# Leaving the first product of a column block whole instead of dividing it into two column parts

## The reference

```
proj   = rms_norm(x) @ w_in                    # 1024 -> 10 x 1024
y_conv = (silu(zc) * bg * conv(cg * xc)) @ w_out_conv
y_attn = (silu(za) * attention(q, k, v)) @ w_out_attn
x      = rms_norm(x + (g_conv * y_conv + g_attn * y_attn) @ w_o)
for layer in (0, 1):                           # second block
    mix = concat(attention(x @ w_in...), memory_attention(x, mem)) @ w_out
    x   = layer_norm(ALPHA * x + mix)
    a, b = split(x @ ffn_w_in)                 # 1024 -> 2 x 2816
    x   = layer_norm(ALPHA * x + (gelu(conv(a)) * b) @ ffn_w_out)   # 2816 -> 1024
```

## Time and profile before

| | |
|---|---|
| time, median of 3 runs | 921.16 us (921.1 to 921.88) |
| time of the profiled execution | 921.2 us |
| its span, first to last instruction | 919.5 us |
| mean granted TensorE clock | 0.997 |
| PE busy | 906.9 us, 99% of the span |
| VectorE (DVE), ScalarE (ACT) busy | 648.1 us, 524.4 us |
| divided first products recorded (L1684) | 36 |

### The profile page before, as it was taken

One profiled execution on the slowest core, in us unless ns is written; L12 is line 12 of the kernel. 1 busy time (PEld: TensorE's weight loads), 2 busy tenths in 40 slices (PEclk: granted clock), 3 DMA queues, 4 the chain that ended last, 5 costly groups with the idle time before them and its releaser, 6 DMA issues.

```text
span 919.5 us, 19487 instructions
## 1 busy us (share of the span) xinstructions
PE 906.9 (99%) x6993; PEld 835.3 (91%) x6994; DVE 648.1 (70%) x1240; ACT 524.4 (57%) x975; POOL 54.7 (6%) x101
## 2 busy tenths in 40 slices
PE   8999999999999999999999999999999999999996
PEld 6899999999999998878999999999888799999995
DVE  6766676666766777867876666677677877666666
ACT  6645555555544569856655545565666565555554
POOL 2100000000000003401000000000000100000000
PEclk9999999999999999999999999999999999999998
DMA  7665555555766872326456555555554455655541
GB/s 258 218 204 174 182 170 185 178 199 191 250 207 213 320 257 93 121 93 206 162 195 238 182 196 191 195 196 182 190 174 155 160 184 194 239 184 186 200 160 46
DMA packets 48380, 173.02 MB, mean 188 GB/s; under 512 B 6047, under 2 KB 6495, under 8 KB 48204
## 3 DMA queue, kind: packets, MB, share of 16 engines
q1 hardware_dynamic: 44732, 159.73, 51.6%
q0 software_dynamic: 3456, 12.61, 4.4%
q10 hardware_dynamic: 144, 0.04, 0.0%
HBM read 171.29 MB, written 1.07 MB: 187 GB/s over the span
## 4 chain that ended last, share of the span: by engine, by line
PE 96%; ACT 1%; DVE 1%; issue 0%; POOL 0%; DVEq 0%; POOLq 0%; ACTq 0%
PE banks L1688 19%; PE banks L1689 19%; PE banks L1687 19%; PE ysum L1758 7%; PE ysum L1759 7%; PE ysum L1760 7%; PE banks L1809 2%; PE ysum L1816 2%; PE ysum L1823 2%; PE ysum L1872 1%; PE ysum L1878 1%; PE ysum L1875 1%; PE banks L1700 1%; PE banks L1705 1%; PE banks L1701 1%; PE ysum L1798 1%
## 5 line engine op out<-in xcount | busy, mean ns | idle before, releaser
L1688 PE MATMUL banks<-sb_xl,sb_wh 128*128 128x256 f32 x1360 | 378.1, 278 | 0.0
L1689 PE MATMUL banks<-sb_xh,sb_wl 128*128 128x256 f32 x1360 | 376.0, 276 | 0.0
L1687 PE MATMUL banks<-sb_xh,sb_wh 128*128 128x256 f32 x1332 | 370.0, 278 | 0.0
L982 DVE TENSOR_TENSOR sb_wl<-sb_raw,sb_wh 128x1024 fp32r<-128x1024 f32 x192 | 234.4, 1222 | 96.3 <-ACT sb_wh L514 95.4
L1689 PEld LDWEIGHTS banks<-sb_xh,sb_wl 128*128 128x128 f32 x1360 | 255.7, 188 | 0.0
L1688 PEld LDWEIGHTS banks<-sb_xl,sb_wh 128*128 128x128 f32 x1360 | 255.4, 188 | 0.0
L1687 PEld LDWEIGHTS banks<-sb_xh,sb_wh 128*128 128x128 f32 x1332 | 250.1, 188 | 3.8 <-issue 3.6
L514 ACT ACTIVATE sb_wh<-sb_raw 128x1024 fp32r<-128x1024 f32 x192 | 201.7, 1055 | 89.4 <-PE banks L1689 42.2
L1758 PE MATMUL ysum<-sb_wh,sb_mh 128*128 128x512 f32 x208 | 81.3, 391 | 0.1
L1759 PE MATMUL ysum<-sb_wl,sb_mh 128*128 128x512 f32 x208 | 81.1, 390 | 0.0
L1760 PE MATMUL ysum<-sb_wh,sb_ml 128*128 128x512 f32 x208 | 81.0, 390 | 0.0
(11 more groups left out here) (335 smaller groups left out, 1471.1 us busy)
## 6 DMA issues: line engine op xcount, KB each, us to landing
sb_raw<-in_stream SPq DMA_DIRECT2D x197, 512.0 KB, 3.8
sb_gates<-in_stream SPq DMA_DIRECT2D x63, 512.0 KB, 3.3
sb_t_dg<-in_stream SPq DMA_DIRECT2D x32, 512.0 KB, 4.1
sb_bias<-rel_rows POOLq DMA_DIRECT2D x9, 384.0 KB, 3.7
sb_bias<-in_alibi POOLq DMA_DIRECT2D x8, 256.0 KB, 3.1
sb_gb<-in_ln_g POOLq DMA_DIRECT2D x4, 512.0 KB, 4.8
sb_gb<-in_ln_b POOLq DMA_DIRECT2D x4, 512.0 KB, 6.6
sb_blk<-rel_rows POOLq DMA_DIRECT2D x3, 384.0 KB, 4.0
```

The source lines that it names most:

```text
L982: dve.tensor_tensor(wl[slot][:, :, :], raw[home_of(b)][:, :, :], wh[slot][:, :, :].bitcast(F32), ALU.subtract).then_inc(split_l, 1)
L1687: pe.matmul(out, wh[slot][:, k, :], mov_h(k), start=k == 0, stop=False)
L1688: pe.matmul(out, wh[slot][:, k, :], mov_l(k), start=False, stop=False)
L1689: last = pe.matmul(out, wl[slot][:, k, :], mov_h(k), start=False, stop=k == KT - 1)
```

## The change

The three callers no longer ask for a split. The code of `stationary` is the same, and its branch with L1684 and L1685 is never taken.

```diff
-                    stationary(slot_of(B_FIRST + p), bank[p % 3][:, 0:T], xm, xml, made=made if p == 0 else None, split=P if kind == "ga" else 0)
+                    stationary(slot_of(B_FIRST + p), bank[p % 3][:, 0:T], xm, xml, made=made if p == 0 else None)
...
-                        column(n, slot_of(b0 + 5 + n), SPLIT if n == 0 else 0)
+                        column(n, slot_of(b0 + 5 + n), 0)
...
-                    stationary(slot_of(pair_at(n)), bk[:, 0:T], xm, xml, split=P if n > 2 else 0)
+                    stationary(slot_of(pair_at(n)), bk[:, 0:T], xm, xml, split=0)
```

## The result

The changed kernel takes 928.21 us (927.76 to 929.55, 6 runs), the kernel before 921.16 us (920.75 to 921.88). The ratio is 1.0074, with a 95% interval of 1.0064 to 1.0083: **slower by 7.05 us**, where 3.9 us faster had been forecast, and outside the range.

What follows compares the result with a forecast made beforehand. The prediction took PE to bound the kernel. Gains of 2.76 us behind row blocks, 0.84 between column blocks, 0.11 in the last pass of `first` and 0.22 in the attention summed to 3.93: 921.2 to 917.3 us, range 916.5 to 919.3.

Steps and rivals of the forecast that it cites:

- What bounds the kernel: Whole kernel: PE is the bound, busy for 99% of the span and 96% of the chain.
- The price of a split at rest, 0.12 us: Column blocks: a split block takes 2.84 us, an undivided one 2.72, so each split removed gains 0.12 us.
- The attention: Five splits in the attention: three ahead of PE's wait gain nothing, two behind it gain 0.22 us.
- The supply: Weights for PE's products: paced by PE itself, expected to move along; thinnest repeating cover 0.35 us, in `first`.
- behind a row block: First products of 23 batches: removing each split gains 0.12 us, 2.76 us in all.
- The lower bound of 0.08 us: Batches behind row blocks: least gain per split removed, before correcting for the `sb_memh` slot; 1.84 us for 23.
- The stall belongs to the seam: Rival, behind row blocks: whole first products have the 0.22 us gap too, the 23 give nothing; 920.0 us, chance 8%.
- The slower rival: Rival, in `first`: low weights come late, PE waits 1.0 us in each of seven passes; 924.3 us, chance 4%.

Runs made afterwards that it cites:

- e4: Kernel before, all splits kept, but in a batch's first column block the product of k = 4 is divided, not k = 0: 922.55 us, +0.9.
- e12: Changed kernel with the low-weight product second and the low-activation product third in all dense column blocks: 927.4 us against 921.82 for the kernel before.
- e14: e8, with the last product also halved in row blocks that end a stage: 919.25 us against 921.51 for the kernel before.
- e2: Kernel before with whole first products in the batches alone, splits kept in projection and attention: 928.05 us against 921.62.
- e3: Kernel before, all splits kept, but in a batch the second column block is divided, not the first: 924.19 us, +2.6.
- e1: Kernel before with the split kept in the batches alone, whole products in projection and attention: 921.04 us against 921.62.
- e8: Changed kernel with the last 512-column product of the row block ahead of a batch done as 256 + 256: 919.79 us against 921.26 for the kernel before.
- e13: Changed kernel with one 512-column product of a batch's row blocks halved, at another place in each stage: 927.44 us against 921.51 for the kernel before.
- e9: As e1, with first parts of 32, 208 and 224 columns in the three stages' batches: 924.87 us against 921.82 for the kernel before.

## Why the prediction was wrong

*What bounds the kernel* was right: PE is the bound, and every nanosecond of its slots is paid.

*The price of a split at rest, 0.12 us,* was right between two column blocks: the whole block takes 2.72 us instead of 2.84. *The attention* went as forecast up to its wait: PE's two waits for `sb_pt` there grew from 1.3 to 1.6 us in all, and its load behind the longer one starts at 369.30 instead of 368.54 us, 0.76 later, as late as PE had come into the attention (338.61 instead of 337.86). It was the shorter wait that grew, though; the one of 1.11 us is 1.12. Of the 0.22 us behind the wait only some 0.03 came (429.60 instead of 428.87 us at the next stage end), since the block at 380.72 us took the slow slot. *The supply* stayed ahead, as assumed: the trace of the kernel after has no wait of a MATMUL on L1687 to L1689 or L1758 to L1760.

**The step that failed** is the one behind a row block: "the whole one there has other operands (`sb_memh`), with a slot of 0.118 us throughout, against 0.1133 in our blocks. Corrected for nine slots [...] it comes to 0.12 us again." The difference of 0.0045 us was taken for a property of the operands and taken out of the sum. It was the effect itself. e4 shows both slots in one block with the same operands, and e12 the slow one with another order of them. e14 has the prediction's own comparison: the same `sb_memh` products at 0.113 us. Left in, it reads: 4 blocks × 24 products × 0.0045 = 0.43 us lost a batch, 0.12 won, 23 × 0.31 = 7.1 us slower, where a gain of 2.76 had been forecast. The trace shows 16.75 instead of 16.45 us a batch, 6.8 us in all, and e2 measured 6.4. That the whole difference, 7.05 us, is as near to 7.1 is luck, since the rest of the kernel moved both ways. The lower bound of 0.08 us was no bound either, since it counted nine slots of 96. And the check that would have caught it was a view already in use: cut into blocks, the kernel before has whole column blocks of 2.83 us at 71.39 us, with our own operands.

*The rivals* missed the mechanism. "The stall belongs to the seam" had the right place and asked whether the first gap stays; it doesn't. No rival asked whether the products behind it keep their pace. *The slower rival* was the supply of `first`, which had no part in it. The Trainium skill (TensorE: Matmul & The Clock Gate, Back-to-back issue gap) gives a lone product's gap as its columns over 2.4 plus 2.5 ns. An estimate from that, 2.5 ns for a split, falls short both ways: the runs show 0.12 us for the split and 0.0045 us for each product behind it.

**What stays open** is why. Shown: there are two slots, they hold themselves over the 96 products of a batch's columns and more, a load in the slow one takes 192 ns instead of 188 once in three, a whole product behind undivided row blocks gave the slow one in all 23 batches of each kernel that had them (after, e2, e3, e4, e12), and additions at the seam gave the fast one or not, by sizes without an order. The slow slot can also end with nothing added: at the stage end at 428.08 us of e1 it does so after six products, behind whole 512-column products, where in the kernels before and after it goes on. That fits a relation of some nanoseconds between the stream and the loads, which repeats with the three products of a group; no run here shows such a relation itself, and none changed the timing at the seam without changing the products.

## What to carry to other kernels

Where PE is the bound, read the distance between the starts of its products, block by block, over the whole kernel, and look for two values; mean durations (281 against 278 ns for L1687 here) and busy shares (99% in both kernels) hardly show it. An instruction that only costs time in the place where it stands may set the pace of a hundred others behind it, so price its removal from a place where the stream *behind* it is the same too. And where a row's slot differs from yours, find out why before correcting for it: here a product of 512 columns halved at the seam (e8, e14) gives the good pace in all 23 batches for 0.03 us, where the split paid 0.12. It does not at two other seams, so such a repair has to be looked up in the trace, place by place.

## What the runs showed of the hardware

- Products of 128 x 128 weights and 256 columns, each with its own load, run at 0.113 or 0.118 us a product at a granted clock of 1.00, 2.72 or 2.83 us a column block: 4%. Either can last for nine blocks (216 products, the slow one in e9).
- Dividing a product in two costs 0.12 us between 256-column products (2.84 against 2.72 us a block), and 0.03 us on a 512-column product (16.78 against 16.75 us a batch, e13).
- The seam behind attention's small products gives either slot: the fast one at most passes, the slow one at 68.46 us of the kernel before and at 246.53 us of the kernel after.
